# A modulation matvec split over two feed-forward stages, folded over partitions on VectorE, with its gate rows spread later

## What is computed

```python
mod = silu(c) @ ada_w + ada_b                    # (1,1024) @ (1024,6144): no token in it
sh1, sc1, g1, sh2, sc2, g2 = split(mod, 6)
h = rmsnorm(x, norm_mix_g) * (1 + sc1) + sh1
x = x + g1 * conformer_conv(h, ...)              # projection, 31-tap conv, layer norm, projection
h = rmsnorm(x, norm_ffn_g) * (1 + sc2) + sh2
x = x + g2 * hier_moe(h, ...)                    # 32 experts, 192 MB of weights
out = rmsnorm(x, final_g)
```

## Time and profile before

| | |
|---|---|
| median of 3 runs | 1475.56 us (1472.04 to 1477.86) |
| profiled execution, first to last instruction (span) | 1473.6 us |
| what the median has on top of that span | 2.0 us |
| PE busy / PE weight loads / DVE / ACT / POOL | 89% / 61% / 51% / 31% / 3% |
| granted TensorE clock, mean | 0.938 |
| HBM read | 353.63 MB, 241 GB/s over the span |

### The profile page before, as it was taken

One profiled execution on the slowest core, in us unless ns is written; L12 is line 12 of the kernel. 1 busy time (PEld: TensorE's weight loads), 2 busy tenths in 40 slices (PEclk: granted clock), 3 DMA queues, 4 the chain that ended last, 5 costly groups with the idle time before them and its releaser, 6 DMA issues.

```text
span 1473.6 us, 16820 instructions
## 1 busy us (share of the span) xinstructions
PE 1315.1 (89%) x6278; PEld 903.2 (61%) x6278; DVE 745.1 (51%) x1520; ACT 450.9 (31%) x731; POOL 39.4 (3%) x80
## 2 busy tenths in 40 slices
PE   5979999989977789999887895779999998999995
PEld 4867888876745677888766884654444343344332
DVE  3675555566647669998784998431111111111113
ACT  4424444445443244444442643211001000011001
POOL 0000000000000001221000000000000000000000
PEclk8989999999986699999987998779999999999998
DMA  7345555633530268899551320689999999999993
GB/s 255 116 144 197 174 172 182 207 124 115 177 131 1 86 219 290 304 313 317 211 172 58 115 86 1 261 332 362 336 408 405 404 407 409 409 406 404 407 408 124
DMA packets 179465, 355.42 MB, mean 241 GB/s; under 512 B 7418, under 2 KB 63411, under 8 KB 179410
## 3 DMA queue, kind: packets, MB, share of 16 engines
q1 hardware_dynamic: 172066, 327.96, 60.3%
q0 software_dynamic: 6912, 25.17, 5.0%
q10 hardware_dynamic: 432, 1.57, 0.3%
HBM read 353.63 MB, written 1.05 MB: 241 GB/s over the span
## 4 chain that ended last, share of the span: by engine, by line
PE 62%; DVE 16%; DMA 14%; SPq 4%; ACT 3%; issue 1%; DVEq 0%; ACTq 0%
DMA odd_expert<-in_moe_w_up 13%; PE ps L385 13%; PE ps L387 12%; PE ps L386 12%; PE ps L2345 11%; DVE xn L2001 4%; PE ps L2374 3%; SPq L561 3%; DVE w_lo L359 2%; PE ps L2334 2%; PE ps L2383 1%; DMA dense_weights<-in_ev_w_in 1%; PE ps L1855 1%; SPq L988 1%; DVE ada_acc L1834 1%
## 5 line engine op out<-in xcount | busy, mean ns | idle before, releaser
L359 DVE TENSOR_TENSOR w_lo<-dense_weights,w_hi 128x1024 fp32r<-128x1024 f32 (+1 forms) x228 | 270.6, 1209 | 142.9 <-ACT w_hi L354 142.5
L354 ACT CAST w_hi<-dense_weights 128x1024 fp32r<-128x1024 f32 (+1 forms) x228 | 233.7, 1038 | 277.1 <-PE ps L387 240.9
L385 PE MATMUL ps<-w_hi,xT_lo 128*128 128x512 f32 (+1 forms) x624 | 252.4, 405 | 35.2 <-DVE xT_lo L2036 12.9
L386 PE MATMUL ps<-w_lo,xT_hi 128*128 128x512 f32 (+1 forms) x624 | 246.8, 396 | 0.0
L387 PE MATMUL ps<-w_hi,xT_hi 128*128 128x512 f32 (+1 forms) x624 | 246.8, 395 | 0.0
L385 PEld LDWEIGHTS ps<-w_hi,xT_lo 128*128 128x128 f32 x624 | 121.1, 194 | 64.8 <-issue 19.0
L387 PEld LDWEIGHTS ps<-w_hi,xT_hi 128*128 128x128 f32 x624 | 120.7, 193 | 25.9
L386 PEld LDWEIGHTS ps<-w_lo,xT_hi 128*128 128x128 f32 x624 | 121.2, 194 | 24.6 <-issue 0.5
L2345 PE MATMUL ps<-odd_expert,ge_xT 128*64 128x512 f32 x480 | 108.0, 603 | 15.9 <-DMA odd_expert<-in_moe_w_up 15.9
L2463 DVE COPY ge_y<-ps 128x512 f32<-128x512 f32 x32 | 22.1, 692 | 197.7 <-PE ps L2374 197.7
L2468 DVE SCALAR_TENSOR_TENSOR ge_a<-ge_th,ps 128x256 f32<-128x256 f32 x32 | 13.5, 421 | 206.3 <-ACT ge_th L2420 206.3
(11 more groups left out here) (376 smaller groups left out, 1747.0 us busy)
## 6 DMA issues: line engine op xcount, KB each, us to landing
dense_weights<-in_moe_w_gate SPq DMA_DIRECT2D x16, 2048.0 KB, 16.6
...
```

The source lines that it names most:

```text
L354: act.copy(split_view(w_hi, name, i, j), piece(name, i, j)).then_inc(hi_ready, 1)
L359: dve.tensor_tensor(split_view(w_lo, name, i, j), piece(name, i, j), split_view(w_hi, name, i, j).bitcast(F32), ALU.subtract).then_inc(pie ...
L385: pe.matmul(out, left[1], right[0], start=start, stop=False)
L386: pe.matmul(out, left[0], right[1], start=False, stop=False)
```

## The change

The products are taken in twelve blocks of 512 columns and no longer in ffn1 and ple1, but after DVE's steps 0, 1, 3, 5, 7 and 9 of both ffn0 and ffn1. A block is one DMA of 2 MB into one of two buffers, 8 dependent multiply-adds of 128x512, a transpose of each 32x32 square (`ada_accT`) and a sum over the 32 elements of each square's row: 16 columns of `mod_parts`. What is left to sum over are the four groups of 32 partitions: four small matmuls with `fold` (128x32) between the halves of ple1. All six vectors come out as columns, with one bias addition. The two gate vectors are spread into rows later: POOL multiplies `ident` by each gate column (16 squares, `gate_diag`), four matmuls with `ones` follow the layer norm's last sum on PE, and ACT copies the rows into `g_bc`.

```diff
--- before.py
+++ after.py
-ADA_BUFFERS = 4
+ADA_BUFFERS = 2
+ADA_COLS = 512
+ADA_BLOCKS = 6 * D // ADA_COLS
...
-        mod_cols = sb("mod_cols", [P, 4, KC])
+        mod_cols = sb("mod_cols", [P, 6, KC])
...
+            mod_parts = dense("mod_parts", [P, 6 * D // 32])
+            fold = dense("fold", [P, 32])
...
-                ada_acc = st("ada_acc", [P, 6 * D])
-                ada_w = st("ada_w", [P, ADA_BUFFERS, KC // 2, BLK])
+                ada_acc = st("ada_acc", [P, ADA_COLS])
+                ada_accT = st("ada_accT", [P, ADA_COLS])
+                ada_w = st("ada_w", [P, ADA_BUFFERS, KC, ADA_COLS])
...
+                gate_diag = st("gate_diag", [P, 2, KC, P])
...
-                    if self.side is not None and n < FF_BLOCKS - 1:
-                        self.side(dve, n, it)
+                    if n in ADA_AT:
+                        ada_products(dve, ADA_PER_LAYER * self.layer + ADA_AT.index(n), it)
...
+                    if i == 1 and self.between is not None:
+                        pe.wait_ge(self.between.cols, 1)
...
+                    if i == 0 and self.between is not None:
+                        self.between.pe_sums(pe)
...
-                        self.side(dve, i)
+                    if i == 1 and self.between is not None:
+                        self.between.dve_cols(dve, own)
...
+                own(dve.tensor_tensor(fold[:], ident[:, 0:32], ident[:, 32:64], ALU.add))
+                for q in (2, 3):
+                    own(dve.tensor_tensor(fold[:], fold[:], ident[:, 32 * q:32 * (q + 1)], ALU.add))
...
-        def ada_loads(pool):
-            w = a["ada_w_2"][0].rearrange("(s k p) n -> p s k n", p=P, s=2)
...
-            with pool.Fori(1, ADA_ITEMS // ADA_BUFFERS) as it:
-                for q in range(ADA_BUFFERS):
-
-                    pool.wait_ge(ada_used, ADA_BUFFERS * it + q // 2 * 2 - 2)
-                    load(q, it)
...
+        ADA_AT = (0, 1, 3, 5)
+        ada_steps, ada_parts = sem("ada_steps"), sem("ada_parts")
+        def ada_loads(pool, layer):
+            w = a["ada_w_2"][0].rearrange("(k p) n -> p k n", p=P)
+            pool.wait_ge(h_ready, 2 if layer == 0 else 8)
+            for j in range(ADA_PER_LAYER * layer, ADA_PER_LAYER * (layer + 1)):
+                if j >= ADA_BUFFERS:
+                    pool.wait_ge(ada_used, j - ADA_BUFFERS + 1)
+                pool.dma_start(ada_w[:, j % ADA_BUFFERS], w[:, :, j * ADA_COLS:(j + 1) * ADA_COLS]
+                               ).then_inc(ada_landed[j % ADA_BUFFERS], 16)
+        def ada_products(dve, j, it):
+            dve.wait_ge(ada_landed[j % ADA_BUFFERS], per_round(16 * (j // ADA_BUFFERS + 1), it, 16))
+            for k in range(KC):
+                w, c_col = ada_w[:, j % ADA_BUFFERS, k], c_act[:, k:k + 1]
+                if k == 0:
+                    ins = dve.tensor_scalar(ada_acc[:], w, c_col, None, ALU.mult)
+                else:
+                    dve.wait_ge(ada_steps, per_round(KC * j + k, it, 2 * KC))
+                    ins = dve.scalar_tensor_tensor(out=ada_acc[:], in0=w, scalar=c_col, in1=ada_acc[:], op0=ALU.mult, op1=ALU.add)
+                ins.then_inc(ada_steps if k < KC - 1 else ada_used, 1)
+            dve.wait_ge(ada_used, per_round(j + 1, it, 2))
+            dve.transpose(ada_accT[:], ada_acc[:]).then_inc(ada_steps, 1)
+            dve.wait_ge(ada_steps, per_round(KC * (j + 1), it, 2 * KC))
+            n = ADA_COLS // 32
+            sums = mod_parts[:, bass.ds(per_round(n * j, it, 2 * n), n)]
+            dve.tensor_reduce(sums, ada_accT[:].rearrange("p (b i) -> p b i", i=32), AX.X, ALU.add).then_inc(ada_parts, 1)
...
-            def load(self, act):
-                for i, v in enumerate(self.ROWS):
-                    act.dma_start(g_bc[:, i], a["ada_b_2"][0, v * D:(v + 1) * D].partition_broadcast(P)
-                                  ).then_inc(self.b_landed, 16)
-            def pe(self, pe):
-                pe.wait_ge(h_ready, 12)
-                pe.wait_ge(ada_used, ADA_ITEMS)
-                for i, v in enumerate(self.COLS):
-                    for c in range(KC):
-                        last = pe.matmul(ps[:, 0, i * KC + c:i * KC + c + 1], ada_acc[:, v * D + c * P:v * D + (c + 1) * P],
-                                         ones[:, 0:1], start=True, stop=True)
+                self.diag, self.spread = sem("mod_diag_made"), sem("mod_spread")
+            def pe_sums(self, pe):
+                pe.wait_ge(ada_parts, ADA_BLOCKS)
+                parts = mod_parts[:].rearrange("p (n q) -> p q n", q=4)
+                for q in range(4):
+                    last = pe.matmul(ps[32 * q:32 * (q + 1), 7, 0:6 * KC], fold[:], parts[:, q], start=True, stop=True)
                 last.then_inc(self.summed, 1)
-                for i, v in enumerate(self.ROWS):
-                    for j in range(2):
-                        last = pe.matmul(ps[:, 4 + 2 * i + j, :], ones[:], ada_acc[:, v * D + j * 512:v * D + (j + 1) * 512],
-                                         start=True, stop=True)
-                last.then_inc(self.summed, 1)
-                pe.wait_ge(self.cols, 1)
             def dve_cols(self, dve, own):
                 dve.wait_ge(self.summed, 1)
-                for i, v in enumerate(self.COLS):
-                    own(dve.tensor_tensor(mod_cols[:, i], ps[:, 0, i * KC:(i + 1) * KC], col("ada_b_2", v * KC, KC), ALU.add))
-                for i, name in ((1, "norm_mix_g_2"), (3, "norm_ffn_g_2")):
+                own(dve.tensor_tensor(mod_cols[:].rearrange("p v c -> p (v c)"), ps[:, 7, 0:6 * KC], col("ada_b_2", 0, 6 * KC), ALU.add))
+                for i, name in ((self.SCALE1, "norm_mix_g_2"), (self.SCALE2, "norm_ffn_g_2")):
                     last = dve.scalar_tensor_tensor(out=mod_cols[:, i], in0=mod_cols[:, i], scalar=1.0, in1=col(name, 0, KC),
                                                     op0=ALU.add, op1=ALU.mult)
                 last.then_inc(self.cols, 1)
                 dve.wait_ge(self.cols, 1)
-            def dve_rows(self, dve):
-                dve.wait_ge(self.summed, 2)
-                dve.wait_ge(self.b_landed, 32)
+            def pool(self, pool):
+                pool.wait_ge(self.cols, 1)
+                pool.wait_ge(h_ready, 12)
+                for i, v in enumerate((self.GATE1, self.GATE2)):
+                    for c in range(KC):
+                        last = pool.tensor_scalar(gate_diag[:, i, c], ident[:], mod_cols[:, v, c:c + 1], None, ALU.mult)
+                last.then_inc(self.diag, 1)
+            ROW_BANKS = (0, 1, 4, 5)
+            def pe_rows(self, pe):
+                pe.wait_ge(self.diag, 1)
+                for n, bank in enumerate(self.ROW_BANKS):
+                    cols = gate_diag[:, n // 2].rearrange("p c n -> p (c n)")[:, n % 2 * 512:(n % 2 + 1) * 512]
+                    last = pe.matmul(ps[:, bank, :], ones[:], cols, start=True, stop=True)
+                last.then_inc(self.spread, 1)
+            def act_rows(self, act):
+                act.wait_ge(self.spread, 1)
                 for i in range(2):
-                    last = dve.tensor_tensor(g_bc[:, i].rearrange("p (j n) -> p j n", j=2), ps[:, 4 + 2 * i:6 + 2 * i, :],
-                                             g_bc[:, i].rearrange("p (j n) -> p j n", j=2), ALU.add)
+                    bank = self.ROW_BANKS[2 * i]
+                    last = act.copy(g_bc[:, i].rearrange("p (j n) -> p j n", j=2), ps[:, bank:bank + 2, :])
                 last.then_inc(self.rows, 1)
-                dve.wait_ge(self.rows, 1)
...
                 last.then_inc(self.var, 1)
+                mod.pe_rows(pe)
                 for i in range(2):
+                    if i == 1:
+                        pe.wait_ge(mod.rows, 1)
                     tokens_by_columns(pe, "conv_out", i, (2 + 2 * i, 3 + 2 * i), chunks=self.lo)
...
                     act.activation(mixT[:, c], self.y_view[:, c], ACT.Square).then_inc(self.squares, 1)
+                mod.act_rows(act)
                 for c in range(KC):
...
         even = EvenStage()
-        ffn = [FfnStage(0, norms[1]), FfnStage(1, norms[4], ada_products)]
-        ple = [PleStage(0, norms[2]), PleStage(1, norms[5], lambda dve, i: ada_products(dve, FF_BLOCKS - 1 + i, None))]
+        mod = ModStage()
+        ffn = [FfnStage(0, norms[1]), FfnStage(1, norms[4])]
+        ple = [PleStage(0, norms[2]), PleStage(1, norms[5], mod)]
...
-            mod.load(act)
...
             setup.pool(pool)
+            ada_loads(pool, 0)
             odd_in.pool(pool)
             for _ in range(2):
                 stage_end(pool)
-            ada_loads(pool)
+            ada_loads(pool, 1)
+            mod.pool(pool)
             stage_end(pool)
...
-            mod.pe(pe)
...
-            norms[6].dve(dve, own, ("conv_in", 0, 3), lambda eng: mod.dve_cols(eng, own))
-            mod.dve_rows(dve)
+            norms[6].dve(dve, own, ("conv_in", 0, 3))
```

(6 more changed lines are left out.)

43 lines of the change are left out of this document (6 added, 37 removed).

## The result

The changed kernel takes **1480.92 us** (median of 8 runs, 1479.68 to 1484.58), the kernel before 1475.03 us (8 runs, 1470.93 to 1477.86). The ratio is 1.0048 with a 95% interval of 1.0034 to 1.0062: 5.9 us slower, where 11.6 us faster were forecast. The time lies above the whole range.

The account below looks back on a forecast made before the run. PE bounds the feed-forward stages, expert loads the last 522 us, with PE's products in the gap after ple1 on the path. -13.5 - 1.3 + 3.2 = -11.6 us gave span 1462.0, 1464.0 with the median's 2.0; range 1460 to 1469.

Parts of the forecast that it names:

- time saved ahead of them moves them whole: Last 522 us, streaming expert weights: loads are released by what comes before, so earlier savings shift the stretch whole.
- a stretch after 952 us that changes its length: Listed as a sign of a wrong prediction: any stretch after 952 us getting a different length.
- Item 1: Gap after ple1, norm 6: modulation products leave, last write of `h` to first projection falls from 29.1 to 15.6 us; -13.5.
- Item 2: ple1: DVE takes up the last product 2.5 us sooner, against +0.9 for `fold` matmuls and +0.3 column wait; -1.3 us.
- Item 3: Products in ffn0 and ffn1: a block takes 7.4 us, paid at block 0, covered by slack later; +3.2 us.
- Items 4 and 5: Moved `ada_w` loads land in time, two bias loads vanish; gate-row work is covered up to the layer norm's tanh; 0 each.
- Item 6: Norm 6: POOL's 16 squares run beside DVE's 12 small root steps; taken as 0, up to +3.3 us.
- the rival's mechanism: Norm 6: POOL's squares hold DVE's two-input root steps; +1 to +3.3, taken as +2, 1466 us; chance 0.20.
- outgrow the slack: Feed-forward stages: a product block above 7.9 us makes low parts late in later blocks too; 1484 us at 9.5; chance 0.10.
- the bursts: Feed-forward stages: 2 MB loads delay weights behind them, 8 blocks losing 1 us each; 1472 us; chance 0.05.
- a block at 6.6 us: Product block in the feed-forward stages without cost of dependence; the low end of the forecast's own range, -13.5 us.
- the far end of item 3: Feed-forward products with a 9.1 us block, its transpose costing four times its row's elements; +18 us in total.

Follow-up runs that it names:

- experiment 1: Changed kernel with `cols_b` 16 columns smaller, so every tile behind it lies 64 bytes lower, as in the kernel before; 1470.64 us, ratio to before 0.9969.
- experiment 14: Changed kernel with `cols_b` 16 columns smaller and an unused 64-byte tile at the start of the experts' scope, moving only the last stretch's tiles; 1481.2 us.
- experiments 3 and 8: Both expert weight tiles placed at multiples of 512 bytes: 3 in the changed kernel, 1464.09 us; 8 in the kernel before, 1467.04 us.
- experiment 12: Changed kernel with both expert weight tiles and the feed-forward tiles at multiples of 512 bytes and the first product block split; 1454.91 us, ratio 0.9885.
- experiment 4: Changed kernel with `cols_b` 16 columns smaller and POOL's 16 squares started after norm 6's last low part, not when `h` is written; 1468.61 us.
- experiment 6: On experiment 5: first product block of both stages split, three of its eight multiplications moved to where DVE waits for the tanh; 1462.27 us, ratio 0.993.
- experiment 5: On experiment 1: an unused 128-byte tile behind `fold`, so the feed-forward tiles start at a multiple of 512 bytes; 1465.78 us, ratio 0.9952.
- experiment 2: Kernel before with `cols_b` 16 columns larger, so all tiles behind it lie 64 bytes higher, as in the changed kernel; 1485.52 us, ratio 1.0078.
- experiment 7: Kernel before with an unused 384-byte tile ahead of the feed-forward stages' tiles, nothing else moved; 1479.25 us, ratio 1.0041.

## Why the prediction was wrong

- **The step that failed first** is the first part's "time saved ahead of them moves them whole". The last stretch was taken as a block of fixed length because no instruction in it changed. It grew by 13.8 us because its target tile moved by 64 bytes: experiment 1 takes it back (532.2 us), and experiment 14 puts it there again. The sign "a stretch after 952 us that changes its length" was named, but no rival stood behind it, and `mod_cols` going from 4 to 6 vectors stood in the diff.
- **The second step that failed** is the sum of what the change itself does. With the loads' targets in equal places it brought 3 us and not 11.6 (experiments 3 and 8), so the forecast would have missed without the 64 bytes too. By the traces of 3 and 8, the stretches of norm 6 and conformer gave 10.2 us and not 13.5, ple1 1.4, and ffn0 and ffn1 cost 7.2 us and not 3.2. The items below say why. Close to the forecast came only the mended kernel, experiment 12 against 8, with 10 to 12 us.
- **Item 1, -13.5: right in mechanism, not paid out whole.** The gap gave 12.3 us (29.1 - 16.8), and 13.5 once POOL was out of the way (experiment 4). It reached norm 7 with 12.1 in the trace after, but that trace is a good one. Ten traces with early squares and the unsplit block show 161.9 to 166.5 us for this stretch, four of the kernel before 173.8 to 174.6. The spread is mostly the layer norm: PE's wait of 2.4 or 3.9 us and the products at 3.7 or 5.1 to 6.7 us behind it.
- **Item 2, -1.3: right in sum**, -1.4, with parts that are off both ways. DVE takes up the last product 2.2 us sooner, not 2.5 (3.77 us behind its start, against 5.98). The eight small records cost PE 0.5 us and not 0.9, and the wait for the columns 0.3.
- **Item 3, +3.2: the block right, the sum too small**, +8.6. The block takes the 7.4 us forecast, PE pays 1.8 and 1.7 us at block 0 against 0 and 0.7 before, and nothing in the later blocks; experiment 6 takes it back. Not seen were the down products, 400/395/395 ns for 391/389/389, which is 3.4 us over both stages and two thirds of it by the place of their tiles (experiment 5). Nor was, in ffn0, a stretch near half clock right after PE's wait: from 154.9 to 158.9 us the granted clock is 0.57, which costs about 1.7 us. Some 0.4 us per stage stay open. The prediction's estimate for the transpose, worked out from the Trainium skill (Vector Engine (DVE) Microarchitecture Reference, the reshape front-end section: one element per cycle and lane, so 0.53 us and a fixed part), fits the measured 0.71.
- **Items 4 and 5, 0 each: right.** In experiment 6 DVE didn't wait for the 2 MB load, and the layer norm covered the gate rows: `conv_out` starts at 905.27, 9.5 us earlier than before (914.73), as DVE's first convolution chain did (807.8 against 817.2).
- **Item 6, 0: wrong**, +1.2 inside its range, by the rival's mechanism. A square takes 592 ns, not 0.37 us, but of the last nine steps, the ones with two inputs, it holds up only every second for about 0.19 us. The Trainium skill, SBUF — State Buffer, Who interferes with whom, has it that a DVE instruction with two SBUF inputs contends with a GpSimd instruction that reads SBUF, and the trace agrees: 0.16 us each with POOL out of the way (experiment 4), 0.35 for every second beside it. The price was smaller than a whole square for each of nine. The first two steps, which have one input, were held too, 0.31 and 0.30 us against 0.17.
- **Rivals.** The product block did not outgrow the slack, the bursts did not delay weights (moved bytes 237 and 238 GB/s with PE waiting for no load). The change is slower by none of the cases that carried chances. Two ends of the prediction's sums are a little off, without weight: a block at 6.6 us gives -13.2 and not -13.5, and the far end of item 3 is +18.6.

## What to carry to other kernels

Before forecasting an edit that resizes or adds a tile, list the addresses of all tiles in both kernels, and hold the targets of the large loads at multiples of 256 bytes: here that was worth 6 us with one target and 17 us with two, where the edit itself was worth 3 as written and 10 to 12 with its feed-forward tiles and its first block mended. A stretch without a changed instruction is not a constant. And compare two kernels with their tiles in equal places first, else the placement is taken for the effect of the edit.

## What the runs showed of the chip

- Loads of 2 MB into SBUF ran at 413, 407 and 394 GB/s with none, one and both of two alternating targets off a multiple of 256 bytes, at the same DMA share of 1.04. The offsets tried are 0, 64 and 128 bytes for the odd tile and 0, 128 and 256 for the even one.
- The down products (128x512) took 395 instead of 389 ns when the `ff_hidT` tiles lay 384 or 448 bytes past a multiple of 512, and 389 at 0, 64 (experiment 2, with `w_hi` and `w_lo` at 64 too) and 256. Why 64 is free is open. In all the slow kernels the tiles lie 384 bytes, modulo 512, behind `w_hi`'s place, so it may be the distance that counts.
- The granted clock fell to or near half (1.2 of 2.4 GHz) behind short stops of PE in some kernels and not in others with the same instructions: in the layer norm where PE had been idle for 3.9 us (5.1 to 6.8 us for work of 3.7) and not where for 2.4, and in the first 25 us of a feed-forward stage (0.93 in experiment 7, 1.00 in 8). Each such stretch costs 1.5 to 3 us, as much as some of the edits under test, so single traces don't tell these apart.
